# Weights and work buffers moved by 32 bytes in their partitions, and one row sum placed later, in a two-block transformer kernel

## The chip, the cores and the metric

The kernel runs on one core of one Trainium2 chip. The metric is the device time of one execution in microseconds, as the median of several executions. A profiled execution gives besides it a trace of every instruction on the engines: TensorE (PE, with its weight loads shown apart as PEld), VectorE (DVE), ScalarE (ACT), GpSimd (POOL) and SyncE (SP), which issues the DMAs.

## The reference: what is computed

Two small transformer stacks of two layers each, on 256 tokens of width 1024, in float32:

```
for i in range(2):                       # first block
    h = h + mixer_i(rms_norm(h))         # i=0: causal attention with rope (A); i=1: latent attention (B)
    h = h + conv_ffn(rms_norm(h))        # gelu(conv3(x @ w_gate)) * (x @ w_up) @ w_down, inner width 2816
h = rms_norm(h, norm_final)
for i in range(2):                       # second block
    x = x + mixer2_i(rmsnorm(x))         # i=0: pool_mixer (POOL); i=1: chunked attention with a bias (DD)
    x = x + conv_ffn_2(rmsnorm(x))       # silu in place of gelu
```

The pool mixer takes, for each of four groups of 256 channels, a trailing mean over 2, 4, 8 or 16 tokens minus the input, then a 256 by 256 linear map. The four FFNs are called F0, F1, F2 and F3; the order of the stages is A, F0, B, F1, POOL, F2, DD, F3.

## The kernel before, in words

All matrix products run on TensorE in `float32r`. A float32 number is split into a high part (what `float32r` keeps) and a low part (the rest), and each product is the sum of high times high, high times low and low times high. Activations lie channel by channel: `xT` (a part of the tile `gx`) holds the residual stream as 8 chunks of 128 channels by 256 tokens, and `xx` holds for each chunk `k` the high part and behind it the low part, 512 elements together.

**Weights.** The weights come from memory as 180-odd units of up to 128 by 2048 elements, in a fixed order (`unit_plan`). SyncE loads a unit into one of three buffers `raw`; ScalarE writes its high part into one of five buffers `whi` (`hi`, line 1165); VectorE subtracts and writes the low part into one of five buffers `wlo` (`lo`, line 1704); TensorE uses both.

**Matmuls.** Each matmul has a stationary operand (128 by 128, loaded by an LDWEIGHTS) and a moving one. In the FFNs and in half of the output projections the weights are stationary. `block_wide` (lines 458 and 460) is the pair of matmuls that does nearly all of this: the high weights against high and low activations together (512 moving elements), then the low weights against the high activations (256). Its moving operand is `xx` for the gate and up products, `hx` (the FFN's hidden activations, split the same way) for the down product, and `ox` (the attention output) for two of the four output units of each mixer. In one FFN there are 11 x 2 units x 8 chunks x 2 halves = 352 such pairs on `xx`, and 3 x 22 x 2 + 22 = 154 on `hx`; in each of the three attention mixers 32 on `ox`. That is 1408, 616 and 96 pairs in all. In the query, key and value products of A and DD (`high` and `low`, lines 671, 672 and 678) it is the other way round: the activations `xx` are stationary, and the weights `whi` or `wlo` are moving, 512 elements at a time, 3 x 192 = 576 matmuls. `three` (lines 417 to 419) is used elsewhere: three matmuls, of 256 moving elements as a rule.

**Order.** Every engine has its own program, written out by hand, and the engines meet at semaphores: `s_res` (a chunk pair of the residual stream is final), `s_xh` and `s_xl` (high and low part of a chunk of `xx` are written), `s_hs` (the row sums are split), `s_sum`, `s_sr`, `s_used` (TensorE has finished with a unit).

**The norm.** In an FFN the gate and up products run on activations without their norm, and the factor per token is multiplied in afterwards. The sum of squares over channels goes through `ssum` and its split copy `sx` (high by ScalarE line 1230, low by VectorE `low_sums`, line 1761) and is spread over all partitions by two matmuls with a matrix of ones (`spread_sums`, lines 512 to 514). VectorE reads the result from the bank `SB` (`norm_spread`, line 1767) and takes the inverse square root. A "row" of the FFN here is one index `i`: a gate unit and an up unit, 256 of the 2816 hidden channels.

**From POOL to F2.** While TensorE ends the pool mixer, VectorE and ScalarE finish the residual stream chunk by chunk: `normed(k)` (VectorE, line 2255) applies the final norm of the first block, `averages(g)` (line 2262) adds the pool mixer's output to chunks 2g and 2g+1, `split_x(F2, k)` writes chunk `k` of `xx` (ScalarE the high part, line 1168, VectorE the low part, line 1709). F2 starts on chunks 0 and 1 alone, gate and up, and goes on chunk by chunk.

**Addresses.** `sb` places tiles one behind another in each partition, in the order of the calls, at multiples of 32 bytes. In the built program `raw0` starts at byte 1152, a multiple of 64. All tiles but `gx` (8224 bytes) and `vec` (1756 bytes, 1760 with its filling) have a length that is a multiple of 64 up to the FFN's buffers, so the place of a tile within a 64-byte line changes only behind these two. Every slice that a wide matmul reads starts a multiple of 512 bytes behind its tile's start, so it has its tile's place in the line.

Of the kernel before, what the change touches and what calls it, by code (L numbers as in the profile page):

```python
# [100 lines left out]
def build(nc, dram, out):  # L101
    plan, first = unit_plan()
    N_UNITS = len(plan)
    with ExitStack() as ctx:
        def sb(name, shape, dt=F32, stack=ctx):
            return stack.enter_context(nc.sbuf_tensor(name, shape, dt))

        def sem(name):
            return ctx.enter_context(nc.semaphore(name))

# [38 lines left out]
        s_dv, s_ac = sem("s_dv"), sem("s_ac")  # L149

        raw = [sb(f"raw{i}", [128, UNIT]) for i in range(RAW)]
        whi = [sb(f"whi{i}", [128, UNIT], F32R) for i in range(RING)]
        wlo = [sb(f"wlo{i}", [128, UNIT], F32R) for i in range(RING)]
        gx = sb("gx", [128, KD + KD * S])
        xT = gx[:, KD:].rearrange("p (k s) -> p k s", k=KD)
        xx = sb("xx", [128, KD, 2, S], F32R)
        con = sb("con", [128, CON_N])
        vec = sb("vec", [128, VEC_N])
        ones = sb("ones", [128, 128])
        ones_r = sb("ones_r", [128, 128], F32R)  # L160
# [254 lines left out]
        def tensor_program(e):  # L415
# [47 lines left out]
            def across_wide(n, b, k, a, kk, start, stop):  # L463
                block_wide(n, b[:, 0, :], 0, k, a, kk, start, stop)
                return block_wide(n, b[:, 1, :], 1, k, a, kk, start, stop)
# [57 lines left out]
            def ffn(s):  # L523
                u = first[s]
                bg, bu = ffn_banks(s, 0), ffn_banks(s, 1)
                weights_here(u + 1)
                if s != F2:
                    e.wait_ge(s_res, n_res(s - 1, 1))
                if s == F2:
                    for k in (0, 1):  # L530
                        x_here(s, k)
                        across_wide(u, bg, k, xx, k, k == 0, False)
                    e.wait_ge(s_uu, 2)
                    for k in (0, 1):
                        across_wide(u + 1, bu, k, xx, k, k == 0, False)
                for k in range(2 if s == F2 else 0, KD):
                    x_here(s, k)
                    last = across_wide(u, bg, k, xx, k, k == 0, k == KD - 1)
                    if k == KD - 1:
                        last.then_inc(s_used, 1)  # L540
                    last = across_wide(u + 1, bu, k, xx, k, k == 0, k == KD - 1)
                    if k == KD - 1:
                        last.then_inc(s_used, 1)
                spread_sums(s)
                for i in range(1, 11):
                    n = u + 2 * i
                    bg, bu = ffn_banks(s, 2 * i), ffn_banks(s, 2 * i + 1)
                    weights_here(n)
                    if i >= 2:
                        e.wait_ge(s_gr, n_ff(s, i - 2))  # L550
                    for k in range(KD):
                        last = across_wide(n, bg, k, xx, k, k == 0, k == KD - 1)
                    last.then_inc(s_used, 1)
                    weights_here(n + 1)
                    if i >= 2:
                        e.wait_ge(s_ub, n_ff(s, i - 2))
                    else:
                        e.wait_ge(s_sr, LAYER[s] + 1)
                    for k in range(KD):
                        last = across_wide(n + 1, bu, k, xx, k, k == 0, k == KD - 1)  # L560
                    last.then_inc(s_used, 1)
                n = u + 22
                for c in range(4):
                    b = ffn_banks(s, 2 + c)
                    e.wait_ge((s_gr, s_ub)[c % 2], n_ff(s, 9 + c // 2))
                    if c == 3:
                        last_pair(s)
                        break
                    k0 = 0
                    for j, nk in enumerate((8, 8, 6)):  # L570
                        weights_here(n)
                        for k in range(nk):
                            if c == 0:
                                e.wait_ge(s_hl, n_ff(s, (k0 + k) // 2))
                            last = across_wide(n, b, k, hx, k0 + k, k0 + k == 0, k0 + k == NF - 1)
                        last.then_inc(s_used, 1)
                        n += 1
                        k0 += nk
# [1109 lines left out]
        def vector_program(e):  # L1688
# [548 lines left out]
            def pool_mixer():  # L2237
                s = POOL
                u = first[s]
                e.wait_ge(s_sum, s + 1)  # L2240
                sums = SB[:, 0, 0:4].rearrange("p (h w) -> p h w", h=2)
                e.tensor_scalar(va[:, 0:2], sums[:, :, 0], 1.0 / D, EPS, ALU.mult, ALU.add)
                kept(e.tensor_scalar(va[:, 2:4], sums[:, :, 1], 1.0 / D, None, ALU.mult))
                after_own()
                kept(e.scalar_tensor_tensor(out=va[:, 2:4], in0=va[:, 0:2], scalar=EPS, in1=va[:, 2:4], op0=ALU.mult,
                                            op1=ALU.add))
                rsqrt(va, ra, ta).then_inc(s_rc, 1)
                norm_diag(s, ra)
                norm_row(s, 0)
                e.wait_ge(s_rb, ROW[s])  # L2250
                e.wait_ge(s_xh, n_x(s, KD - 1))

                def normed(*chunks):
                    for k in chunks:
                        kept(e.scalar_tensor_tensor(out=xT[:, k, :], in0=xT[:, k, :], scalar=vcol("norm_final", k),
                                                    in1=rb[:, :], op0=ALU.mult, op1=ALU.mult))

                def averages(g):
                    xp = xT[:, 2 * g:2 * g + 2, :]
                    e.wait_ge(s_uu, g + 1)  # L2260
                    after_own()
                    e.tensor_tensor(xp, xp, pu[:, 2 * g:2 * g + 2, :], ALU.add).then_inc(s_res, 1)

                normed(0, 1, 2)
                averages(0)
                normed(3, 4)
                split_x(F2, 0)
                split_x(F2, 1)
                averages(1)
                normed(5)  # L2270
                split_x(F2, 2)
                split_x(F2, 3)
                normed(6, 7)
                averages(2)
                add_squares(F2, 1)
                split_x(F2, 4)
                split_x(F2, 5)
                averages(3)
                add_squares(F2, 2)
                split_x(F2, 6)  # L2280
                split_x(F2, 7)
                add_squares(F2, 3)
                fold_sums(F2)
                lo(u + 3)
                low_sums(F2)
                lo(u + 4)
# [177 lines left out]
```

## Time and profile before

| | us |
|---|---|
| median of 3 executions (1076.17 to 1076.5) | 1076.34 |
| profiled execution, its own time | 1077.13 |
| span of the profiled execution, first to last instruction | 1075.3 |
| PE busy / DVE busy / ACT busy | 1068.8 / 838.6 / 655.7 |

The span is what the trace covers; the execution's own time has 1.8 us around it. Busy time of PE is a sum over modelled ends of pipelined matmuls, so the time between the starts of two matmuls that follow each other says more than the duration of one. It is called a slot below. The granted TensorE clock is 1.000 of full speed over the span (its upper level, 2.4 GHz).

### The profile page before, as it was taken

The numbers are of one execution on the slowest core, as the hardware profiler recorded it, in microseconds if no ns is written. First come the engines' busy times: TensorE is split into PE (matmuls) and PEld (weight loads), VectorE is DVE, ScalarE is ACT, GpSimd is POOL, SyncE is SP. The second block draws the span as 40 slices with busy tenths as digits, with TensorE's granted clock in tenths as the row PEclk, the third lists the DMA queues.
The fourth block names the chain that finished last, engine by engine and source line by source line (L and its number), as shares of the span: only waits on it lengthen the run. The fifth ranks groups of instructions, "written<-read, shape, count | busy, mean of one in ns | idle before, by whom it ended". The sixth has DMA issues, their size and how long they took to land.

```text
span 1075.3 us, 16292 instructions
## 1 busy us (share of the span) xinstructions
PE 1068.8 (99%) x6536; PEld 934.0 (87%) x6536; DVE 838.6 (78%) x1364; ACT 655.7 (61%) x922; POOL 1.3 (0%) x8
## 2 busy tenths in 40 slices
PE   9999999999999999999999999999999999999998
PEld 7778888888898888888889888888877788888887
DVE  7985799877668778987767999776658768997852
ACT  7656567655467765766456577654456765776540
POOL 0000000000000000000000000000000000000000
PEclk9999999999999999999999999999999999999999
DMA  8553356555427154655552366555555434655530
GB/s 304 200 188 119 130 184 230 202 186 215 144 83 270 41 186 168 229 206 183 213 193 101 135 222 231 186 216 186 180 182 181 151 118 148 235 215 191 206 142 30
DMA packets 32092, 191.67 MB, mean 178 GB/s; under 512 B 4497, under 2 KB 6161, under 8 KB 12177
## 3 DMA queue, kind: packets, MB, share of 16 engines
q1 hardware_dynamic: 32016, 190.62, 49.9%
q8 instruction: 52, 0.85, 0.3%
q14 instruction: 24, 0.19, 0.0%
HBM read 189.56 MB, written 1.05 MB: 177 GB/s over the span
## 4 chain that ended last, share of the span: by engine, by line
PE 95%; DVE 2%; ACT 1%; DMA 1%; issue 1%; SPq 0%; DVEq 0%; ACTq 0%
PE banks L458 21%; PE TB L458 12%; PE SB L458 12%; PE banks L460 11%; PE SB L460 6%; PE TB L460 6%; PE banks L671 4%; PE banks L678 4%; PE banks L672 4%; PE banks L417 3%; PE banks L419 3%; PE banks L418 3%; PE banks L628 2%; PE TB L602 2%; PE SB L589 1%; DMA raw<-in_a_first 1%
## 5 line engine op out<-in xcount | busy, mean ns | idle before, releaser
L1704 DVE TENSOR_TENSOR wlo<-raw,whi 128x2048 fp32r<-128x2048 f32 (+2 forms) x180 | 395.9, 2201 | 76.2 <-ACT whi L1165 75.9
L1165 ACT ACTIVATE whi<-raw 128x2048 fp32r<-128x2048 f32 (+2 forms) x180 | 330.4, 1839 | 81.1 <-PE TB L460 25.6
L458 PE MATMUL banks<-xx,whi 128*128 128x512 f32 x752 | 262.1, 390 | 0.0
L460 PE MATMUL banks<-xx,wlo 128*128 128x256 f32 x752 | 212.0, 282 | 0.0
L458 PEld LDWEIGHTS banks<-xx,whi 128*128 128x128 f32 x752 | 141.1, 188 | 29.6
L460 PEld LDWEIGHTS banks<-xx,wlo 128*128 128x128 f32 x752 | 142.1, 189 | 0.0
L458 PE MATMUL TB<-xx,whi 128*128 128x512 f32 x336 | 117.7, 390 | 0.3 <-DVE xx L1709 0.3
L458 PE MATMUL SB<-xx,whi 128*128 128x512 f32 x320 | 111.8, 390 | 0.0
L460 PE MATMUL TB<-xx,wlo 128*128 128x256 f32 x336 | 94.7, 282 | 0.0
L458 PE MATMUL banks<-hx,whi 128*128 128x512 f32 x264 | 91.7, 391 | 0.0
L460 PE MATMUL SB<-xx,wlo 128*128 128x256 f32 x320 | 90.2, 282 | 0.0
L1250 ACT ACTIVATE ct<-gp,vec 128x256 f32<-128x256 f32 x88 | 48.2, 595 | 63.4 <-DVE gp L1871 63.4
L671 PE MATMUL banks<-whi,xx 128*128 128x512 f32 x192 | 78.6, 409 | 1.1 <-ACT whi L1657 1.1
L672 PE MATMUL banks<-whi,xx 128*128 128x512 f32 x192 | 76.3, 398 | 0.0
L458 PEld LDWEIGHTS TB<-xx,whi 128*128 128x128 f32 x336 | 63.0, 188 | 13.6 <-issue 0.5
L460 PE MATMUL banks<-hx,wlo 128*128 128x256 f32 x264 | 73.9, 280 | 0.0
L458 PEld LDWEIGHTS SB<-xx,whi 128*128 128x128 f32 x320 | 60.0, 188 | 12.6
L460 PEld LDWEIGHTS TB<-xx,wlo 128*128 128x128 f32 x336 | 63.5, 189 | 0.0
L458 PE MATMUL TB<-hx,whi 128*128 128x512 f32 x176 | 61.2, 391 | 0.0
L458 PE MATMUL SB<-hx,whi 128*128 128x512 f32 x176 | 61.2, 391 | 0.0
L460 PEld LDWEIGHTS SB<-xx,wlo 128*128 128x128 f32 x320 | 60.5, 189 | 0.0
L458 PEld LDWEIGHTS banks<-hx,whi 128*128 128x128 f32 x264 | 49.4, 187 | 10.8
(244 smaller groups left out, 1949.0 us busy)
## 6 DMA issues: line engine op xcount, KB each, us to landing
raw<-in_gate SPq DMA_DIRECT2D x44, 1024.0 KB, 4.8
raw<-in_up SPq DMA_DIRECT2D x44, 1024.0 KB, 4.8
raw<-in_down SPq DMA_DIRECT2D x32, 1024.0 KB, 4.8
raw<-in_down SPq DMA_DIRECT2D x16, 768.0 KB, 4.2
raw<-in_d_kq SPq DMA_DIRECT2D x8, 1024.0 KB, 4.9
raw<-in_a_kq SPq DMA_DIRECT2D x6, 1024.0 KB, 5.2
raw<-in_a_o SPq DMA_DIRECT2D x4, 1024.0 KB, 4.9
raw<-in_b_o SPq DMA_DIRECT2D x4, 1024.0 KB, 5.4
```

Source lines behind the costliest of these rows:

```text
L417: e.matmul(po, ah, bh, start=start, stop=False, skip_group_check=True)
L418: e.matmul(po, ah, bl, start=False, stop=False, skip_group_check=True)
L419: return e.matmul(po, al, bh, start=False, stop=stop, skip_group_check=True)
L458: e.matmul(po[:, 0:512], wh[:, k, sl], a[:, kk, :, :].rearrange("p w s -> p (w s)"), start=start, stop=stop, skip_group_check=True)
L460: return e.matmul(po[:, 0:256], wl[:, k, sl], a[:, kk, 0, :], start=False, stop=stop, skip_group_check=True)
L602: last = e.transpose(TB[:, a, c * 128:(c + 1) * 128], sc[:, a, c * 128:(c + 1) * 128], ident)
L671: e.matmul(po, xx[:, k, 0, sl], wh[:, k % 4, :], start=k == 0, stop=False, skip_group_check=True)
L672: e.matmul(po, xx[:, k, 1, sl], wh[:, k % 4, :], start=False, stop=False, skip_group_check=True)
L678: return e.matmul(slot_bank(s, i, h)[:, :], xx[:, k, 0, sl], wl[:, k % 4, :], start=False, stop=k == KD - 1, skip_group_check=True)
L1165: e.activation(whi[n % RING][:, 0:nk * w], raw[n % RAW][:, 0:nk * w], ACT.Copy).then_inc(s_hi, 1)
L1250: e.activation(ct[:, m, :], g[:, m, 0:S], ACT.Identity, scale=cw(0, 2 * i + m), bias=cb(2 * i + m)).then_inc(s_tap, 1)
L1704: e.tensor_tensor(wlo[n % RING][:, 0:nk * w], raw[n % RAW][:, 0:nk * w], whi[n % RING][:, 0:nk * w].bitcast(F32), ALU.subtract).then_inc(s ...
```

## The change

Three unused tiles of 32 bytes are allocated between others (`off_line`), which moves what lies behind them. In bytes from the last multiple of 64, as the built programs have it:

| tile | before | after |
|---|---|---|
| `raw0` to `raw2` | 0 | 0 |
| `whi0` to `whi4`, `wlo0` to `wlo4` | 0 | 32 |
| `gx`; `xT` in it | 0; 32 | 0; 32 |
| `xx`, `con` | 32 | 32 |
| `vec` | 32 | 0 |
| `ones`, `ones_r`, `sx`, `sq`, `ssum`, `rb`, `small`, `dg`, `crs`, `rtmp` | 0 | 32 |
| `hx`, `gp0`, the FFN's other buffers | 0 | 32 |
| `gp1` | 32 | 0 |
| `ox`, `vv`, `sc`, `pt`, `qT`, `kT` and the mixers' other buffers | 0 | 32 |

So for the wide matmuls the places of moving and stationary operand go, from (32, 0) to (32, 32) for `xx` against weights; from (0, 0) to (32, 32) for `hx` and `ox` against weights; and from (0, 32) to (32, 32) for weights against `xx`.

Apart from that, `spread_sums` of F2 is issued after the first chunk of the gate product of row 1 and no longer before that row, and VectorE does `normed(4)` after `averages(1)`.

```
+        def off_line(name):
+
+            sb(f"pad_{name}", [128, 8])
+
         raw = [sb(f"raw{i}", [128, UNIT]) for i in range(RAW)]
+        off_line("weights")
         whi = [sb(f"whi{i}", [128, UNIT], F32R) for i in range(RING)]
         wlo = [sb(f"wlo{i}", [128, UNIT], F32R) for i in range(RING)]
+        off_line("tokens")
         gx = sb("gx", [128, KD + KD * S])
         xT = gx[:, KD:].rearrange("p (k s) -> p k s", k=KD)
         xx = sb("xx", [128, KD, 2, S], F32R)
         con = sb("con", [128, CON_N])
+        off_line("moving")
         vec = sb("vec", [128, VEC_N])
...
-                spread_sums(s)
+                if s != F2:
+                    spread_sums(s)
                 for i in range(1, 11):
...
                     for k in range(KD):
                         last = across_wide(n, bg, k, xx, k, k == 0, k == KD - 1)
+                        if s == F2 and i == 1 and k == 0:
+                            spread_sums(s)
...
                 normed(0, 1, 2)
                 averages(0)
-                normed(3, 4)
+                normed(3)
                 split_x(F2, 0)
                 split_x(F2, 1)
                 averages(1)
-                normed(5)
+                normed(4, 5)
```

The order of TensorE at the end of the eight chunks of F2's row 0, before the change (the last four matmuls of row 0, the two of `spread_sums`, the first of row 1):

```order
L458 MATMUL banks<-xx,whi 128x512
L460 MATMUL banks<-xx,wlo 128x256
L458 MATMUL banks<-xx,whi 128x512
L460 MATMUL banks<-xx,wlo 128x256
L513 MATMUL SB<-sx,ones_r 128x256
L514 MATMUL SB<-sx,ones_r 128x256
L458 MATMUL banks<-xx,whi 128x512
```

And of the changed kernel, from the same place on (its `block_wide` has lines 465 and 467, its `spread_sums` line 520 and the one after it):

```order
L465 MATMUL banks<-xx,whi 128x512
L467 MATMUL banks<-xx,wlo 128x256
L465 MATMUL banks<-xx,whi 128x512
L467 MATMUL banks<-xx,wlo 128x256
L465 MATMUL banks<-xx,whi 128x512
L467 MATMUL banks<-xx,wlo 128x256
L465 MATMUL banks<-xx,whi 128x512
L467 MATMUL banks<-xx,wlo 128x256
L520 MATMUL SB<-sx,ones_r 128x256
```

Four matmuls of row 1 now stand ahead of the two that read `sx`.

The order of VectorE from the copy of the norm's row on, before (x3 and x2: that many in a row; 2255 is `normed`, 2262 `averages`, 1709 `split_x`):

```order
L1780 COPY rb<-TB 128x256
L2255 SCALAR_TENSOR_TENSOR gx<-gx,vec,rb 128x256 x3
L2262 TENSOR_TENSOR gx<-gx,pu 128x512
L2255 SCALAR_TENSOR_TENSOR gx<-gx,vec,rb 128x256 x2
L1709 SCALAR_TENSOR_TENSOR xx<-gx,vec,xx 128x256 x2
L2262 TENSOR_TENSOR gx<-gx,pu 128x512
L2255 SCALAR_TENSOR_TENSOR gx<-gx,vec,rb 128x256
L1709 SCALAR_TENSOR_TENSOR xx<-gx,vec,xx 128x256 x2
```

And of the changed kernel (2265, 2272 and 1719 are the same three):

```order
L1790 COPY rb<-TB 128x256
L2265 SCALAR_TENSOR_TENSOR gx<-gx,vec,rb 128x256 x3
L2272 TENSOR_TENSOR gx<-gx,pu 128x512
L2265 SCALAR_TENSOR_TENSOR gx<-gx,vec,rb 128x256
L1719 SCALAR_TENSOR_TENSOR xx<-gx,vec,xx 128x256 x2
L2272 TENSOR_TENSOR gx<-gx,pu 128x512
L2265 SCALAR_TENSOR_TENSOR gx<-gx,vec,rb 128x256 x2
L1719 SCALAR_TENSOR_TENSOR xx<-gx,vec,xx 128x256 x2
```

One `normed` stands two places later, behind the second `averages`. No instruction is added, removed or resized on any engine, and the orders are the same everywhere else.

## Rows read from the trace of the kernel before

**Rows 1.** The page's first part: span; busy us, share of the span, instructions.
```profile
span 1075.3 us, 16292 instructions
PE 1068.8 (99%) x6536; PEld 934.0 (87%) x6536; DVE 838.6 (78%) x1364; ACT 655.7 (61%) x922; POOL 1.3 (0%) x8
```
**Rows 2.** The chain of work that ended last, shares of the span by engine.
```profile
PE 95%; DVE 2%; ACT 1%; DMA 1%; issue 1%; SPq 0%; DVEq 0%; ACTq 0%
```
**Rows 3.** Waits of PE: total us, times, longest us.
```profile
PE SB L513 <- DVE sx L1761: 0.5, 1, 0.5
```
**Rows 4.** Groups of PE: out<-moving,stationary, count, busy us, mean ns, idle before.
```profile
L458 PE MATMUL banks<-xx,whi 128*128 128x512 f32 x752 | 262.1, 390 | 0.0
L458 PE MATMUL banks<-hx,whi 128*128 128x512 f32 x264 | 91.7, 391 | 0.0
L671 PE MATMUL banks<-whi,xx 128*128 128x512 f32 x192 | 78.6, 409 | 1.1 <-ACT whi L1657 1.1
```
**Rows 5.** Timeline of PE in F0 (start us, us): row 1's start, down's start, its last pair.
```profile
134.00 0.39 PE L458 MATMUL TB<-xx,whi 128*128 128x512 f32 x1
...
244.94 0.39 PE L458 MATMUL TB<-hx,whi 128*128 128x512 f32 x1
...
297.99 0.39 PE L458 MATMUL banks<-hx,whi 128*128 128x512 f32 x1
```
**Rows 6.** Timeline of PE in A's output projection, three pairs apart.
```profile
115.25 0.40 PE L458 MATMUL SB<-ox,whi 128*128 128x512 f32 x1
...
116.31 0.40 PE L458 MATMUL SB<-ox,whi 128*128 128x512 f32 x1
```
**Rows 7.** Timeline of PE at DD's start: the first and the 46th matmul.
```profile
773.10 0.40 PE L671 MATMUL banks<-whi,xx 128*128 128x512 f32 x1
...
783.60 0.40 PE L672 MATMUL banks<-whi,xx 128*128 128x512 f32 x1
```
**Rows 8.** Timeline of PE in B, weights moving against `ox`: 17 slots apart.
```profile
331.00 0.39 PE L419 MATMUL banks<-whi,ox 128*128 128x512 f32 x1
...
334.85 0.39 PE L418 MATMUL banks<-wlo,ox 128*128 128x512 f32 x1
```
**Rows 9.** Timeline of PE, 256 moving: 3 slots apart in F0, 6 apart in POOL.
```profile
300.00 0.28 PE L419 MATMUL banks<-hx,wlo 128*128 128x256 f32 x1
...
300.36 0.28 PE L419 MATMUL banks<-hx,wlo 128*128 128x256 f32 x1
...
580.77 0.28 PE L419 MATMUL banks<-whi,xx 128*128 128x256 f32 x1
...
581.48 0.28 PE L419 MATMUL banks<-whi,xx 128*128 128x256 f32 x1
```
**Rows 10.** Timelines of PE and DVE round `spread_sums` of F2.
```profile
599.80 0.28 PE L460 MATMUL banks<-xx,wlo 128*128 128x256 f32 x1
600.55 0.35 PE L513 MATMUL SB<-sx,ones_r 128*128 128x256 f32 x1 [0.47 <-DVE sx L1761]
600.86 0.39 PE L458 MATMUL banks<-xx,whi 128*128 128x512 f32 x1
...
606.42 0.39 PE L458 MATMUL SB<-xx,whi 128*128 128x512 f32 x1
...
599.99 0.42 DVE L1761 TENSOR_TENSOR sx<-ssum,sx 128x256 fp32r<-128x256 f32 x1
...
602.55 0.41 DVE L1767 TENSOR_SCALAR rtmp<-SB 128x256 f32<-128x256 f32 x1
```
**Rows 11.** Timelines of PE, DVE and ACT at the start of F2.
```profile
588.74 0.47 PE L458 MATMUL TB<-xx,whi 128*128 128x512 f32 x1 [0.31 <-DVE xx L1709]
...
588.12 0.88 DVE L1709 SCALAR_TENSOR_TENSOR xx<-gx,vec,xx 128x256 fp32r<-128x256 f32 x2
...
590.17 0.88 DVE L1709 SCALAR_TENSOR_TENSOR xx<-gx,vec,xx 128x256 fp32r<-128x256 f32 x2 [0.18 <-ACT xx L1168]
...
587.44 0.91 ACT L1168 ACTIVATE xx<-gx,vec 128x256 fp32r<-128x256 f32 x2 [0.28 <-DVE gx L2262]
```

More of the change, by code:

```diff
@@ L106, in sb, with off_line @@
             return stack.enter_context(nc.sbuf_tensor(name, shape, dt))
+        def off_line(name):
+            sb(f"pad_{name}", [128, 8])
         def sem(name):
@@ L151, in build @@
         raw = [sb(f"raw{i}", [128, UNIT]) for i in range(RAW)]
+        off_line("weights")
         whi = [sb(f"whi{i}", [128, UNIT], F32R) for i in range(RING)]
         wlo = [sb(f"wlo{i}", [128, UNIT], F32R) for i in range(RING)]
+        off_line("tokens")
         gx = sb("gx", [128, KD + KD * S])
@@ L157, in build @@
         con = sb("con", [128, CON_N])
+        off_line("moving")
         vec = sb("vec", [128, VEC_N])
@@ L543, in ffn @@
                         last.then_inc(s_used, 1)
-                spread_sums(s)
+                if s != F2:
+                    spread_sums(s)
                 for i in range(1, 11):
@@ L552, in ffn @@
                         last = across_wide(n, bg, k, xx, k, k == 0, k == KD - 1)
+                        if s == F2 and i == 1 and k == 0:
+                            spread_sums(s)
                     last.then_inc(s_used, 1)
@@ L2265, in pool_mixer @@
                 averages(0)
-                normed(3, 4)
+                normed(3)
                 split_x(F2, 0)
@@ L2269, in pool_mixer @@
                 averages(1)
-                normed(5)
+                normed(4, 5)
                 split_x(F2, 2)
```

## The prediction, made before the changed kernel was run

> **What bounds the kernel now.** I read the page's first part, then the chain, then the waits of TensorE. TensorE is busy for 1068.8 of 1075.3 us [rows 1], and 95% of the chain that ended last is TensorE's own work [rows 2]. Its waits for other engines are single ones of 1.1 us at most [rows 3, 4]; the largest inside the change's reach is 0.5 us for `sx` [rows 3]. So nothing but TensorE's own rate, and two places round F2, can move the time: what VectorE, ScalarE and the DMA queue gain or lose by new addresses is hidden unless it is several per cent of a stage. The groups give the forms of the matmuls, but their durations are modelled (390, 391 and 409 ns, which overlap) [rows 4]; the slots between starts are what the time consists of, so I take them from the timeline.
>
> **The slots, by place in the 64 bytes (moving, stationary).**
> - `xx` against weights, (32, 0): rows 1 to 10 of F0 are 10 x 2 x 8 x 2 = 320 pairs, from 134.00 to 244.94 us [rows 5]: 346.7 ns a pair.
> - `hx` against weights, (0, 0): 153 pairs from 244.94 to 297.99 [rows 5]: 346.7 ns a pair.
> - `ox` against weights, the same form and also (0, 0): 3 pairs in 1.06 us [rows 6]: 353.3 ns.
> - weights against `xx`, 512 moving, (0, 32): 45 slots from 773.10 to 783.60 [rows 7]: 233.3 ns.
> - weights against `ox`, 512 moving, (0, 0): 17 slots from 331.00 to 334.85 [rows 8]: 226.5 ns.
> - 256 moving: 120 ns at (0, 0) and 118 ns at (0, 32) [rows 9].
>
> Three things are to be seen. The steady slots differ by steps of 6.7 ns. The same places and the same form have given two of them (`hx` and `ox`), so the place is not all that decides. And the one clean difference at one form is that of the 512-wide single matmuls: 6.8 ns less where both operands start at the same place than where they don't. No matmul of the kernel before has (32, 32), which is what all wide ones get. Its price must be bounded from its neighbours.
>
> **The change, part by part.**
>
> *The queries, keys and values of A and DD*, 576 matmuls of 512 moving elements, go from (0, 32) to (32, 32). If what counts is whether the two operands stand alike, they take the slot of rows 8: 576 x 6.8 ns = 3.9 us less. Lower bound of the cost: that. Upper bound: nothing gained, 0. I take the first, since rows 7 and 8 are the only two of one form that differ in nothing else that I can name. TensorE waits for nobody there but at A's start (1.1 us in all of line 671 [rows 4]), so the gain would be kept.
>
> *The pairs on `xx`*, 1408 of them, go from (32, 0) to (32, 32), *those on `hx`*, 616, and `ox`, 96, from (0, 0). `xx` and `hx` have the same 346.7 ns at unlike and at like places, so I cost both at nothing. The bounds are one step to each side. `ox` shows that one step up exists: 1408 x 6.7 = 9.4 us for `xx` alone. One step down has not been seen for a pair; it would be 2024 x 6.7 = 13.5 us for `xx` and `hx`.
>
> *`spread_sums` of F2.* The last matmul ahead of it starts at 599.80, so TensorE is free at 599.92, a slot of about 118 ns later; the sums start at 600.55 and row 1 at 600.86 [rows 10]. The stall is 0.63 us, and what is late is VectorE's `sx`, from 599.99. Two pairs of row 1 (0.69 us) now go ahead: TensorE would be at the sums at 600.61, and `sx` is there by 600.55. What has been done ahead is saved: 0.63 us, and up to 0.69 us if TensorE comes a little earlier. Behind the sums, VectorE's reading of `SB` (602.55, done by 602.96) releases the up product of row 1, which wrote `SB` first at 606.42 and will ask for it 0.7 us earlier, at 605.7: 2.8 us of margin [rows 10].
>
> *`normed(4)` later.* F2's first matmul (588.74) waited for chunk 0 of `xx`, whose low part began at 588.12; ScalarE's high part began at 587.44, two in 0.91 us, so it was there at about 587.9 [rows 11]. VectorE can begin about 0.15 to 0.2 us earlier, and TensorE with it. But the sums of F2 start when `sx` is ready, not when TensorE is, and VectorE's work up to `sx` is the same in sum. So these 0.15 us end in a wait for `sx`, and I count them at nothing. The cost on the other side: chunk 2's low part, before from 590.17, comes up to 0.44 us (half of a 0.88 us row) later, ready by 591.1; TensorE wants it eight pairs after its start, 588.6 + 2.8 = 591.4 [rows 11]. Hidden, with 0.3 us to spare; without that cover it costs at most 0.2 us. If VectorE's chain to `sx` ends 0.2 us later, so does the gain shrink to 0.5. I take 0.7 for both edits together, bounds 0.4 and 0.9.
>
> **Sum.** 0.7 + 3.9 = 4.6 us. The profiled execution took 1077.13 us with a span of 1075.3, so it would be 1072.5, with a span of 1070.7. The median is 0.8 us below the profiled one: 1076.34 - 4.6 = 1071.7 us. Of a change of this kernel, 0.2% (2.2 us) is about what a measurement can tell from none.
>
> **Rivals.**
> - *Only the sums' place counts: 1075.6 us.* The slots don't depend on the place by 32 bytes, rows 7 and 8 differ for another reason (rows 5 and 6 differ at the same places, which speaks for it), and 0.7 us is left. The Trainium skill (SBUF — State Buffer, Specifications) says that SBUF has 16-byte lines and that crossing to a new one costs; by that rule 32 bytes are two whole lines and every read crosses as many as before, so it gives this same result. The trace neither shows nor excludes it.
> - *A step down for the pairs: 1071.7 - 13.5 = 1058.2 us.* If (32, 32) is a place of its own in which the loads disturb the moving stream less. For it speaks that a pair takes 346.7 ns while the 256-wide slot alone can be 118: there is room. Against it: no pair of rows 5 and 6 has it. The Trainium skill (TensorE: Matmul & The Clock Gate, Wait — 56ns, not 53.3ns?) gives start to start as columns over 2.4 GHz and about 2.5 ns; that would be 325 ns for a pair, so by this page as well there is room, and the trace is 22 ns above it.
> - *Weights off the 64-byte start as stationary operand cost: 1086 us, slower.* The mechanism is read from rows 7 and 8 the other way: not that the places are unlike, but that the stationary operand starts at 32 makes a 512 slot 6.8 ns longer; rows 9 give 2 ns less for a 256 slot. Then each of the 2120 pairs becomes 4.8 ns longer, 10.2 us, nothing is won in A and DD, and the 0.7 us go off: 1085.8. A form of it is that `xx` takes the longer slot that `ox` has: 1076.34 + 9.4 - 0.7 - 3.9 = 1081.1. It decides as soon as a pair on `xx` is over 2 ns longer. Against it: `xx` and `hx` don't differ, but there the stationary operand is at 0 in both, so they say nothing of it.
>
> **How the numbers follow.** Forecast (A and DD gain, pairs as they are, between 1070 and 1074): 0.36. Only the sums' place: 0.2. A step down for pairs: 0.2; some of their cases, with one of `xx` and `hx` alone, lie between 1058 and 1068. Slower by a pair's longer slot: 0.24. Faster by over 0.2% is the first and the third, 0.56 less a little for a gain in A and DD of under 1.5 us: 0.55. Within 0.2%: 0.2 and that little, 0.21. Slower: 0.24. The range from 1057.5 to 1081.5 leaves out the worse half of the slower case (about 0.13) and what would be better than one step down (0.05). The likeliest case's own range is 1070 to 1074.
>
> **What would show it.** In the changed trace: F0's rows 1 to 10 in 110.9 us and the 153 pairs on `hx` in 53.05 (pairs unchanged); DD's first 45 slots in 10.2 us in place of 10.5 (places alike); 0.31 us from the sums' first matmul to the next of row 1 with no wait of over 0.1 us ahead of it. The prediction is wrong if a pair's slot moves at all, since 1 ns in it is 2.1 us; if DD's slots stay at 233; or if TensorE begins to wait in A or DD, where ScalarE and VectorE would then be the bound.

## The result, and the profile after

The changed kernel takes 1086.13 us (median of 4 runs, 1086.03 to 1086.84) against 1076.38 us before (4 runs, 1076.17 to 1076.5): ratio 1.0093, 95% interval 1.0081 to 1.0106. It is 9.75 us slower, where 4.6 us less was forecast and 1081.5 us was the top of the range. The profiled execution of the kernel before was 0.75 us above its median (1077.13), so the two traces differ by 8.9 us only. All ratios compare executions at a granted clock of 0.998 or more; one of e10's ten ran at 0.851, took 1160.53 us and is left out of them.

The page's first part and the chain of the changed kernel, to be read against [rows 1, 2]:

```profile
span 1084.2 us, 16292 instructions
PE 1078.5 (99%) x6536; PEld 933.0 (86%) x6536; DVE 839.0 (77%) x1364; ACT 656.1 (61%) x922; POOL 1.3 (0%) x8
...
PE 96%; DVE 2%; ACT 1%; issue 0%; DMA 0%; SPq 0%; ACTq 0%; DVEq 0%
```

The span grew by 8.9 us and TensorE's busy time by 9.7. VectorE and ScalarE are busy for 0.4 us more each. The list has no new wait of note; the waits of PE (us in total, times, longest), against [rows 3]:

```profile
PE SB L672 <- DVE ones L2298: 1.1, 1, 1.1
PE banks L681 <- ACT whi L1667: 0.7, 1, 0.7
PE SB L1013 <- DVE small L1941: 0.4, 2, 0.2
PE TB L465 <- DVE xx L1719: 0.2, 1, 0.2
```

The wait for `sx` is gone, as meant. So the time is in TensorE's own slots, and there the groups show the pairs longer (395 ns in place of 390 and 391) and the matmuls of A and DD as they were [rows 4]:

```profile
L465 PE MATMUL banks<-xx,whi 128*128 128x512 f32 x752 | 266.4, 395 | 0.0
...
L465 PE MATMUL banks<-hx,whi 128*128 128x512 f32 x264 | 93.2, 395 | 0.0
...
L681 PE MATMUL banks<-whi,xx 128*128 128x512 f32 x192 | 78.4, 408 | 0.7 <-ACT whi L1667 0.7
```

The slots come from the timeline of PE: row 1's start, the down product's start and its 154th pair, in F0 and then in F3; last DD's first and 46th matmul. They answer to [rows 5, 7].

```profile
133.18 0.40 PE L465 MATMUL TB<-xx,whi 128*128 128x512 f32 x1
...
246.25 0.40 PE L465 MATMUL TB<-hx,whi 128*128 128x512 f32 x1
...
300.31 0.40 PE L465 MATMUL banks<-hx,whi 128*128 128x512 f32 x1
...
907.53 0.40 PE L465 MATMUL TB<-xx,whi 128*128 128x512 f32 x1
...
1019.18 0.39 PE L465 MATMUL TB<-hx,whi 128*128 128x512 f32 x1
...
1072.56 0.39 PE L465 MATMUL banks<-hx,whi 128*128 128x512 f32 x1
...
780.94 0.40 PE L681 MATMUL banks<-whi,xx 128*128 128x512 f32 x1
...
791.44 0.39 PE L682 MATMUL banks<-whi,xx 128*128 128x512 f32 x1
```

- F0: 320 pairs on `xx` in 113.07 us and 153 on `hx` in 54.06: 353.3 ns each, 6.7 more than before. The stretch of 473 pairs is 3.14 us longer. F1 is alike (3.15), and F2 from row 1's third pair on, behind the sums in both kernels (3.11).
- F3: 111.65 and 53.38 us, 348.9 ns each: one third of that step, 1.05 us.
- DD: 45 slots in 10.50 us, 233.3 ns, unchanged.

The four stretches sum to 10.5 us. The rest of the program is 1.6 us shorter (0.8 of it ahead of F0's row 1, 0.6 between F1's last pair and the third pair of F2's row 1): 8.9 us.

### The profile page after: what moved, and what is told of

Same layout as the page of the kernel before. It is cut to its first block, busy times and chain, and to the rows that moved or that the text cites. A ratio compares the mean times of both kernels' runs of the same rounds, so it can differ in the third digit from the quotient of the medians.

```text
span 1084.2 us, 16292 instructions
## 1 busy us (share of the span) xinstructions
PE 1078.5 (99%) x6536; PEld 933.0 (86%) x6536; DVE 839.0 (77%) x1364; ACT 656.1 (61%) x922; POOL 1.3 (0%) x8
## 3 DMA queue, kind: packets, MB, share of 16 engines
HBM read 189.56 MB, written 1.05 MB: 176 GB/s over the span
## 4 chain that ended last, share of the span: by engine, by line
PE 96%; DVE 2%; ACT 1%; issue 0%; DMA 0%; SPq 0%; ACTq 0%; DVEq 0%
PE banks L465 21%; PE TB L465 12%; PE SB L465 12%; PE banks L467 11%; PE TB L467 6%; PE SB L467 6%; PE banks L681 4%; PE banks L688 4%; PE banks L682 4%; PE banks L424 3%; PE banks L425 3%; PE banks L426 3%; PE banks L638 2%; PE TB L612 2%; PE SB L599 1%; PE banks L757 1%
## 5 line engine op out<-in xcount | busy, mean ns | idle before, releaser
L465 PE MATMUL banks<-xx,whi 128*128 128x512 f32 x752 | 266.4, 395 | 0.0
```

Source lines behind the costliest of these rows:

```text
L465: e.matmul(po[:, 0:512], wh[:, k, sl], a[:, kk, :, :].rearrange("p w s -> p (w s)"), start=start, stop=stop, skip_group_check=True)
```

## The experiments

e1, e2, e4, e6 and e7 keep the order of before, e3 keeps its addresses; all the others have the order of the changed kernel. None leaves work out. I describe an address by the **distance**: the start of the moving buffer less that of the stationary one, in bytes of a partition, modulo 256. The starts follow from adding up the buffers in the order of their declarations; every slice that a pair reads begins a multiple of 256 bytes behind its buffer's start, so a distance holds for a whole stretch. Before, weights against `xx` are at 32, against `hx` and `ox` at 0; in the changed kernel all three are at 64, because one pad more lies between the weights and `xx` and two more between the weights and `hx` or `ox`, not because of where in a line each stands.

"Pair" is the slot of a pair on `xx` in F0, from the same two rows as above, 320 pairs apart, in the one execution of each kernel that has a trace; other stages can differ, as the text says. Ratios are to the kernel before, timed on the same chip (1076.2 to 1076.4 us).

| kernel | distance `xx`; `hx`, `ox` | pair, ns | median, us | ratio, 95% |
|---|---|---|---|---|
| before | 32; 0, 0 | 346.7 | 1076.38 | 1 |
| changed | 64; 64, 64 | 353.3 | 1086.13 | 1.0081 to 1.0106 |
| e1 weights alone | 64; 32, 32 | 348.9 | 1079.01 | 1.0015 to 1.0033 |
| e2 buffers behind `con` alone | 32; 32, 32 | 346.7 | 1073.95 | 0.997 to 0.9989 |
| e3 order alone | 32; 0, 0 | 346.7 | 1075.84 | 0.9989 to 1.0006 |
| e4 `xx` moved to 64-byte starts | 64; 64, 64 | 353.3 | 1085.15 | 1.0069 to 1.0097 |
| e5 = e2 + e3 | 32; 32, 32 | 346.7 | 1073.75 | 0.9966 to 0.9986 |
| e6 pads ahead of `wlo`, `gx` and `vec` | high 96, low 64 | 353.3 | 1088.85 | 1.0102 to 1.013 |
| e7 weights 16 bytes in, by buffer | mixed | 350.4 | 1082.72 | 1.0045 to 1.0076 |
| e8 changed, `ox` 32 on | 64; 64, 96 | 353.3 | 1088.55 | 1.0099 to 1.0127 |
| e9 | 128; 128, 128 | 351.1 | 1083.81 | 1.0056 to 1.0086 |
| e10 all 64 on | 32; 32, 32 | 346.7 | 1073.67 | 0.9966 to 0.9986 |
| e11 | 160; 160, 160 | 346.7 | 1074.77 | 0.9978 to 0.9996 |
| e12 | high 16, low 144 | 348.9 | 1079.47 | 1.0018 to 1.0041 |
| e13 changed, `ox` at 32 | 64; 64, 32 | 348.9 | 1081.17 | 1.0028 to 1.0058 |
| e14 changed, one pad less | 32; 32, 32 | 346.7 | 1073.89 | 0.9966 to 0.9986 |
| e15 | 224; 224, 224 | 353.3 | 1088.37 | 1.0095 to 1.0125 |
| e16 | high 48, low 176 | 344.5 | 1069.86 | 0.9928 to 0.9964 |
| e17 | 48; 48, 48 | 350.0 | 1081.33 | 1.0038 to 1.0064 |
| e18 | 176; 176, 176 | 353.3 | 1087.80 | 1.0092 to 1.0123 |

### The change taken apart

e1 adds the pads ahead of `whi` and `gx` alone:
```diff
+        off_line("weights")
         whi = [sb(f"whi{i}", [128, UNIT], F32R) for i in range(RING)]
         wlo = [sb(f"wlo{i}", [128, UNIT], F32R) for i in range(RING)]
+        off_line("tokens")
```


> Kernel before, with only the weights' high and low parts moved by 32 bytes; xx stays at 32, hx and ox at 0, no order changed. Theory S (the stationary operand's place decides, the moving one's does not): pairs on xx and on hx both take 352 to 353 ns in place of 346.7, matmuls of three with weights stationary 117.8 in place of 120, weights moving in A and DD stay at 233.3; in all 1086.8 us, the changed kernel and the 0.7 us of its order. Theory T (both operands must be off the 64-byte start): pairs on xx 352 to 353, those on hx (0, 32) stay at 346.7; about 1083.5 us. Theory M (the moved hx and ox and the other buffers cost it): 1076.4 us.

e2 adds the pad ahead of `vec` alone, e3 the new place of the sums and of `normed(4)` alone:
```diff
+        off_line("moving")
         vec = sb("vec", [128, VEC_N])
```


> Kernel before, with only vec and all behind it moved by 32 bytes (hx, ox, the FFN's and mixers' buffers at 32, weights and xx as before). Theory S: pairs on xx and hx stay at 346.7 ns, 1076.4 us, at most 0.3 us more for the few matmuls of B in which ox is stationary. Theory T: the same. Theory M: about 1086 us, with pairs on hx at 352 ns.

```diff
-                spread_sums(s)
+                if s != F2:
+                    spread_sums(s)
...
+                        if s == F2 and i == 1 and k == 0:
+                            spread_sums(s)
```


> Kernel before, with only the changed order: spread_sums of F2 behind the first chunk of row 1, normed(4) behind averages(1). All theories of places: 1075.7 us, 0.7 us less (0.4 to 0.9), with the sums' first matmul starting when it did, at 600.5 us of the span, and two pairs of row 1 ahead of it. If VectorE's chain to sx comes later by what it lost at chunk 2: 1076.1 us.

The timeline of PE in e1 (F0, first two rows) and in e2 (F0):

```profile
132.77 0.40 PE L464 MATMUL TB<-xx,whi 128*128 128x512 f32 x1
...
244.42 0.39 PE L464 MATMUL TB<-hx,whi 128*128 128x512 f32 x1
```
```profile
132.43 0.39 PE L463 MATMUL TB<-xx,whi 128*128 128x512 f32 x1
...
243.37 0.39 PE L463 MATMUL TB<-hx,whi 128*128 128x512 f32 x1
...
296.41 0.39 PE L463 MATMUL banks<-hx,whi 128*128 128x512 f32 x1
```

e1: 348.9 ns on `xx`, 2.2 more, but 346.7 on `hx`, though the weights are 32 bytes on for both. So it isn't the weights' own place that costs. None of the three times expected came. The traced execution took 1077.43 us, 1.6 less than the median, so the 348.9 ns need not be the slot of all ten. e2 is 2.3 us faster than before with the same 346.7 ns: its gain lies in the shorter forms. With `hx` and `ox` at distance 32 a single 256 slot on `hx` went from 119.8 to 116.7 ns (264 of them), one on `ox` from 123.8 to 121.2 (408), and a pair on `ox` from 353.3 to 347.1 (96): 0.8 + 1.1 + 0.6 = 2.5 us (means over neighbouring starts).

e3 shows what the order is worth. Its PE, and VectorE, at the start of F2's row 1, against [rows 10], behind F0's row 1:

```profile
133.63 0.39 PE L458 MATMUL TB<-xx,whi 128*128 128x512 f32 x1
...
599.34 0.28 PE L460 MATMUL banks<-xx,wlo 128*128 128x256 f32 x1
599.85 0.50 PE L458 MATMUL banks<-xx,whi 128*128 128x512 f32 x1 [0.23 <-DVE wlo L1707]
600.19 0.28 PE L460 MATMUL banks<-xx,wlo 128*128 128x256 f32 x1
...
600.66 0.28 PE L513 MATMUL SB<-sx,ones_r 128*128 128x256 f32 x1
...
600.89 0.40 PE L458 MATMUL banks<-xx,whi 128*128 128x512 f32 x1
...
597.52 2.28 DVE L1707 TENSOR_TENSOR wlo<-raw,whi 128x2048 fp32r<-128x2048 f32 x1
```

The sums no longer wait, but the pairs moved ahead of them do: row 1's gate weights get their low part from 597.52 to 599.80, and TensorE, free at 599.46, starts at 599.85. Before, this was hidden, since TensorE stood at the sums until 600.55 [rows 10]. The third pair of row 1 starts at 600.89, before at 600.86 + 2 x 0.347 = 601.55; that is 0.66 us less, of which 0.37 was there at F0's row 1 (133.63, before 134.00), where the programs are the same. The order is worth 0.3 us, and its time can't be told from no change. In the changed kernel row 1 starts late in the same way, by 0.18 us (its first pair at 605.36, behind a matmul of about 118 ns that starts at 605.06), too little to stand in the list of waits.

### Place or distance

e4 leaves the weights and moves `xx` and what is behind it (pads ahead of `xx` and ahead of `ones`); e5 is e2 and e3 together; e6 was meant to move `wlo` and not `whi`.
```diff
         xT = gx[:, KD:].rearrange("p (k s) -> p k s", k=KD)
+        off_line("x")
         xx = sb("xx", [128, KD, 2, S], F32R)
```


> Kernel before, with xx, con and vec moved to a multiple of 64 bytes and all else left at one, so that all operands of wide matmuls are at (0, 0). Theory S: weights moving against xx in A and DD take 226.5 ns in place of 233.3 (576 matmuls, 3.9 us), pairs on xx stay at 346.7 and the products of 256, 288 and 384 moving in B and POOL shift by a few ns: 1072.5 us. Theory T: A and DD stay at 233.3 and nothing else moves: 1076.4 us. If the pairs on xx took the other slot seen at (0, 0), that of ox: plus 9.4 us, 1082 us.

> The two parts of the change that gained alone, together: vec and all behind it moved by 32 bytes, and the order round F2; weights and xx as before. Theory U (a pair of operands at unlike places, 32 bytes apart modulo 64, has one rhythm of 346.7 ns, whatever went before; at like places there are several, and the one that a stage falls into stays): the gains add, 2.3 and 0.5 us, 1073.4 us, every pair on xx, hx and ox at 346.7. Rival, that the gain of the moved buffers lies in VectorE's or ScalarE's work: the same total, but then pairs and matmuls of three would not account for it.

```diff
         whi = [sb(f"whi{i}", [128, UNIT], F32R) for i in range(RING)]
+        off_line("low")
         wlo = [sb(f"wlo{i}", [128, UNIT], F32R) for i in range(RING)]
+        off_line("tokens")
```


> As the moved buffers alone, but the weights' low parts at 32 too: in a pair the 512 slot has stationary high parts at an unlike place, and the 256 slot stationary low parts at a like one. If the disturbance comes from the load that runs under the moving stream (low parts load under the 512 stream), the 512 slot is the one that changes. If the operand's own place decides, the 256 slot alone changes. Theory U with any like operand enough: pairs at 348.9 or 353.3 ns, 1078 to 1086 us; with both loads needed: 346.7, 1074.0 us.

PE in e4, F0:

```profile
132.72 0.40 PE L464 MATMUL TB<-xx,whi 128*128 128x512 f32 x1
...
245.79 0.40 PE L464 MATMUL TB<-hx,whi 128*128 128x512 f32 x1
```

353.3 ns with both operands on 64-byte starts: the loss of the changed kernel, without its weights moved (four executions, 1084.03 to 1086.18 us). e5, which is the changed kernel without the two pads round the weights, keeps 346.7 and is faster than before. e6 is the slowest of all (means of 231.7 and 121.7 ns for the two slots, before 228.3 and 118.3): both matmuls of a pair become longer. This doesn't tell the operands apart: modulo 64 only the low parts were shifted against `xx`, but modulo 256 the high parts went from 32 to 96 as well as the low ones from 32 to 64.

e7 and e8 were made to tell places apart. e7 took the weights 16 bytes in, with tiles of `UNIT + 16` elements. This was unclean: the tiles are then no multiple of 256 bytes and the distance changes from buffer to buffer (80, 144, 208, 16). Its slots are mixed too, from 346.7 ns (A's `ox`) to 351.2. e8 adds a pad of 32 bytes ahead of `ox` to the changed kernel.
```diff
-        whi = [sb(f"whi{i}", [128, UNIT], F32R) for i in range(RING)]
+        whi = [sb(f"whi{i}", [128, UNIT + 16], F32R)[:, 4:4 + UNIT] for i in range(RING)]
```


> As the moved buffers alone, but the weights' high and low parts start 16 bytes behind a multiple of 64, so 16 bytes ahead of xx, hx and ox. If lines of 16 bytes are what counts, all places are alike and pairs go as at like places: 348.9 to 353.3 ns, 1078 to 1086 us. If the distance modulo 64 counts, it is neither alike nor 32: a slot of its own, between 340 and 353 ns; theory U in its simplest form (anything but alike is one rhythm) says 346.7 and 1074.0 us.

```diff
         att_mem = ExitStack()
+        sb("pad_att", [128, 8], F32, att_mem)
         ox = sb("ox", [128, KD, 2, S], F32R, att_mem)
```


> The changed kernel with ox and the mixers' other buffers moved back to 0, so that ox alone is at an unlike place; xx and hx against weights are at (32, 32) as in the changed kernel. If history decides at like places: ox runs at 346.7 ns, and the pairs on xx in F0 and F1, which follow on it, come into the rhythm of 348.9 that they had with the weights alone moved, and hx after them; F2 follows on POOL and stays at 353.3; about 1081 us. If places alone decide: xx and hx stay at 353.3 in F0 to F2 and only ox gains, 0.6 us: 1085.5 us.

The pad moves `ox` and the mixers' other buffers behind it, and none of those that an F stage reads. e8's `ox` pairs (distance 96) took 350.2 ns, which no theory then held had given, and its F3 took 353.3 ns a pair where the changed kernel has 348.9, with the same addresses in F3. With that the theory of places like and unlike fell, and distance, with a memory of what went before, was put in its place. e9 to e12 test the distance: three pads ahead of `xx` (e9), two ahead of `whi` (e10), four ahead of `gx` (e11); e12 puts the weights into one tile each, 16 bytes in.

```diff
+        off_line("x0")
+        off_line("x1")
+        off_line("x2")
         xx = sb("xx", [128, KD, 2, S], F32R)
```


> New theory V: what counts is the distance from the stationary operand's start to the moving one's, modulo 128 bytes (pairs so far: 32 gave 346.7 ns in every run; 0 gave 346.7 or 353.3; 64 gave 348.9 or 353.3; 96 gave 350.0), not whether they stand alike modulo 64. Here, with the order of the change, all wide matmuls are at distance 0 modulo 128. V: pairs on xx and hx at 346.7 or 353.3 (one of the two), weights moving against xx in A and DD at 226.5 in place of 233.3 (3.9 us), as the 17 slots of B before. With pairs at 346.7: 1072 us; at 353.3: 1086 us. The theory of like places modulo 64: pairs at 353.3 or 348.9 and A and DD at 233.3 as when xx was moved to 0, 1085 us.

```diff
+        off_line("w0")
+        off_line("w1")
         whi = [sb(f"whi{i}", [128, UNIT], F32R) for i in range(RING)]
```


> The moved buffers and the order, and weights, xx and all behind moved on by 64 bytes together: the distances are those of that kernel (32 for pairs), the places modulo 128 are the others. Theory V: every pair at 346.7 ns, 1073.7 us. If the place modulo 128 of either operand decides and not the distance, pairs go to 348.9 or more: over 1078 us.

```diff
+        off_line("t0")
+        off_line("t1")
+        off_line("t2")
+        off_line("t3")
         gx = sb("gx", [128, KD + KD * S])
```


> The moved buffers and the order, with 128 bytes more between the weights and gx: distance 160, which is 32 modulo 128. Theory V: every pair at 346.7 ns, 1073.7 us. If the distance counts modulo 256: a slot not seen so far, or one of 348.9 to 353.3, 1078 us and more.

```diff
+        his, los = (sb(name, [128, RING * UNIT + 32], F32R) for name in ("whi", "wlo"))
+        whi = [his[:, 4 + i * UNIT:4 + (i + 1) * UNIT] for i in range(RING)]
+        wlo = [los[:, 4 + i * UNIT:4 + (i + 1) * UNIT] for i in range(RING)]
```


> The moved buffers and the order, with the weights 16 bytes further on (all high parts behind each other in one tile, all low parts in another, so that each starts 16 bytes behind a multiple of 128): distance 16. Theory V has no number for it: between 346.7 and 353.3 ns a pair, 1073 to 1086 us. If only whole steps of 32 bytes count (the distance rounded down), it goes as distance 0, 346.7 or 353.3.

PE in e9, F0:

```profile
133.04 0.39 PE L466 MATMUL TB<-xx,whi 128*128 128x512 f32 x1
...
245.40 0.40 PE L466 MATMUL TB<-hx,whi 128*128 128x512 f32 x1
```

e10 is the clean one: every operand of a pair 64 bytes on, distance 32 kept, and time and slots are those of e5 to 0.1 us. It is also the changed kernel with the weights alone 32 bytes further on: the two pads ahead of `gx` are both ahead of the weights here, so `gx`, `xx` and all behind stand at the changed kernel's own addresses. PE in e10, F0:

```profile
132.77 0.39 PE L465 MATMUL TB<-xx,whi 128*128 128x512 f32 x1
...
243.71 0.39 PE L465 MATMUL TB<-hx,whi 128*128 128x512 f32 x1
```

346.7 ns in place of 353.3, and 12.5 us less. e9 missed both values expected: 128 gives 351.1 ns where 0 gave 346.7 on `hx` [rows 5] and 353.3 on `ox` [rows 6], so those two aren't alike; 128 is no period. e11 (160) has the 346.7 ns of 32, by another rhythm of the slots (230 and 117, 229 and 118, 228 and 118 ns, where 32 has 228 and 118, 228 and 119, 229 and 118).

### The cause by one pad, and the memory

e14 is the changed kernel without the pad ahead of `gx`; the weights stay where the change put them. e13 is the changed kernel with `ox` at distance 32 (a pad of 56 elements ahead of it, which moves the mixers' other buffers too). e15 has six pads ahead of `gx` and the weights as before.
```diff
-        off_line("tokens")
         gx = sb("gx", [128, KD + KD * S])
```


> The changed kernel without its second pad: weights still at 32 modulo 64, xx and all behind 32 bytes less far on, so that every pair is at distance 32. If the distance is the cause: all pairs at 346.7 ns, 1073.7 us, 12.4 us less than the changed kernel, by one pad. If weights off a multiple of 64 cost anything by themselves: more than 1075 us.

```diff
         att_mem = ExitStack()
+        sb("pad_att", [128, 56], F32, att_mem)
         ox = sb("ox", [128, KD, 2, S], F32R, att_mem)
```


> The changed kernel with ox and the mixers' other buffers moved on by 224 bytes, so that ox is at distance 32 from the weights, as it was with the weights alone moved; xx and hx stay at distance 64. If what went before decides at distance 64: ox at 346.7 ns, then xx in F0, F1 and F3 at 348.9, hx after it too; F2, which follows on POOL, open; 1080 to 1082 us. If not: 353.3 stays in F0 to F2 and only ox and the matmuls of three on it gain: 1085 us.

```diff
+        off_line("t0")
...
+        off_line("t5")
         gx = sb("gx", [128, KD + KD * S])
```


> The moved buffers and the order, with 192 bytes more between the weights and gx: distance 224, which is 32 bytes the other way modulo 256 (96 modulo 128). If only the size of the distance counts: 346.7 ns a pair, 1073.7 us. If it goes as the 96 modulo 128 that ox had once: 350.0 ns, about 1081 us.

PE in e14, F0:

```profile
132.82 0.39 PE L464 MATMUL TB<-xx,whi 128*128 128x512 f32 x1
...
243.77 0.39 PE L464 MATMUL TB<-hx,whi 128*128 128x512 f32 x1
...
296.81 0.39 PE L464 MATMUL banks<-hx,whi 128*128 128x512 f32 x1
```

One pad of 32 bytes less, 12.2 us less, as expected: 346.7 ns for all pairs on `xx` and `hx`, in a kernel with the weights 32 bytes into the 64. Here the weights stay and the moving operands go 32 bytes back; in e10 the moving operands stay and the weights go 32 bytes on. Either takes the loss away, so the cause of the slower result is the distance and not the place of one operand. PE in e13, F0 and F2, row 1's start (in F2 its third pair, behind the sums) and the down product's:

```profile
133.16 0.40 PE L466 MATMUL TB<-xx,whi 128*128 128x512 f32 x1
...
244.81 0.39 PE L466 MATMUL TB<-hx,whi 128*128 128x512 f32 x1
...
601.98 0.40 PE L466 MATMUL banks<-xx,whi 128*128 128x512 f32 x1
...
714.34 0.39 PE L466 MATMUL banks<-hx,whi 128*128 128x512 f32 x1
```

Here F0 takes 348.9 ns and F2 353.3 (318 pairs in 112.36 us), at one distance of 64 and with nothing changed but `ox` and the mixers' buffers behind it, which no F stage reads. The time, 1081.17 us, is the one expected if history decides. At 64 two steady rhythms exist, and F0, with its own addresses unchanged, went from one to the other by a change ahead of it: that is shown; what exactly decides it is not. The four executions of e13 lie within 0.4 us and those of the changed kernel within 0.8, where one stage's other rhythm would be about 2.1 us (473 x 4.4 ns), so in these two it isn't chance from one execution to the next. e15 adds 224, at 353.3 ns in all four F stages, which neither case expected: as high as 64, and unlike 32 or 160. But A's `ox` pairs ran there at 346.7 ns and B's at 353.3, so 224 has two rhythms as well, as 0 has [rows 5, 6].

### Which distance is low

e16 is e12 with one more pad ahead of `gx`. Its expectation and that of e12 call the distance 48 and 16; that is right for the high parts only. Their two tiles are not a multiple of 256 bytes long, so the low parts stood at 176 and 144. I saw this only afterwards; e17 (both tiles 128 bytes longer, both distances 48) and e18 (four more pads, both 176) take the mixture apart.

```diff
+        off_line("t")
         gx = sb("gx", [128, KD + KD * S])
```


> The kernel of distance 16 with 32 bytes more ahead of gx: distance 48, between 32 (346.7 ns, one rhythm) and 64 (348.9 or 353.3). If 32 is the bottom of a slope: about 348 to 350 ns a pair, 1077 to 1081 us. If there is a lower slot still, it would be here: under 346.7.

```diff
-        his, los = (sb(name, [128, RING * UNIT + 32], F32R) for name in ("whi", "wlo"))
+        his, los = (sb(name, [128, RING * UNIT + 64], F32R) for name in ("whi", "wlo"))
```


> The version with the weights 16 bytes into one tile each took 1069.9 us with 344.4 ns a pair, but its distances (moving start less stationary start, modulo 256 bytes) were 48 for the high parts and 176 for the low ones, since its two tiles are not a multiple of 256 bytes long. Here both tiles are 128 bytes longer and both distances are 48. If 48 for the high parts makes the low slot and the low parts count little: 344.4 ns a pair and 1069 to 1071 us, as there. If the distance counts modulo 128 alone: the same. If it was the mixture of 48 and 176 that was low: another slot, 346.7 ns or more, and 1074 us or more.

> As the one with both distances at 48, with 128 bytes more before the tokens, so that both are 176. If the distance counts modulo 128 for this place: 344.4 ns a pair and 1069 to 1071 us, as with 48. If it was 48 for the high parts that was low, and modulo 256 counts (0 and 128 gave 346.7 and 351.1 ns): another slot than 344.4, by the nearest measured ones (160: 346.7, 224: 353.3) 346.7 to 349 ns and 1074 to 1079 us.

PE in F0 of e16, e17 and e18:

```profile
132.56 0.39 PE L465 MATMUL TB<-xx,whi 128*128 128x512 f32 x1
...
242.79 0.39 PE L465 MATMUL TB<-hx,whi 128*128 128x512 f32 x1
```
```profile
135.50 0.40 PE L465 MATMUL TB<-xx,whi 128*128 128x512 f32 x1
...
247.49 0.39 PE L465 MATMUL TB<-hx,whi 128*128 128x512 f32 x1
```
```profile
132.21 0.40 PE L469 MATMUL TB<-xx,whi 128*128 128x512 f32 x1
...
245.27 0.40 PE L469 MATMUL TB<-hx,whi 128*128 128x512 f32 x1
```

344.5, 350.0 and 353.3 ns: 344.4 was one of the values expected for each of the last two, and came in neither. So neither 48 nor 176 is low by itself; only the mixture was. (e17's trace is of its slowest execution, 1083.72 us; it starts F0's row 1 at 135.50, where all other kernels of the table do by 134.0, and the slots behind are steady.) The slot of a pair depends on the distances of its high and of its low part together (or, the same thing said otherwise, also on that between the two weight buffers, 128 in e12 and e16 and 0 elsewhere but in e6 and e7). e16 beats both kernels: 6.5 us less than before and 16.3 less than the changed one. Against e5 it gains 2.2 ns on each of 2120 pairs, 4.7 us, and has 3.9 of them in the median; one of its four executions took 1073.77 us, the others 1070.0 or less.

## Why the prediction was wrong

- **Where the time can come from** held: TensorE's slots alone; VectorE, ScalarE and the waits gave nothing.
- **The step that failed** is "`xx` and `hx` have the same 346.7 ns at unlike and at like places, so I cost both at nothing". That 346.7 ns stood at two distances, 32 and 0, was read as freedom from addresses. The change sent both to a third, 64, which no row of before showed. The upper bound named there, one step of 6.7 ns up, was the truth for three of the four F stages, and not for `xx` alone but for `hx` too: 2024 x 6.7 = 13.5 us at most, of which F3's smaller step (2.2 ns) leaves about 11.2, 10.5 in the stretches measured. It was priced for `xx` alone (9.4 us) and given too little chance.
- **The variable was wrong.** I sorted by each operand's place in 64 bytes. e4 (both at a 64-byte start, slow), e14 (weights 32 in, fast) and e10 (fast with `xx` and `hx` at the changed kernel's addresses) show that the place by itself does nothing. What the change altered was the distance, and a pad ahead of several buffers changes it only towards the buffers on its other side.
- **The rival of 1085.8 us** came within 0.4 us of the time with a mechanism that fell: weights 32 bytes in as the stationary operand cost nothing in e14, nor on `hx` in e1. Its 4.8 ns on each pair stand against 6.7 in three stages and 2.2 in one. The nearness is chance.
- **A and DD, 3.9 us less**: not found, the second term that failed. DD's first 45 slots are 233.3 ns before and after; over all neighbouring starts under 250 ns apart, A and DD both have 233.2 before, and 233.4 and 233.3 after. What made the 226.5 ns of rows 8 short was not that the operands stood alike: both still do in the changed kernel, and the same 17 slots take 233.5 ns there.

```profile
331.08 0.39 PE L426 MATMUL banks<-whi,ox 128*128 128x512 f32 x1
...
335.05 0.40 PE L425 MATMUL banks<-wlo,ox 128*128 128x512 f32 x1
```

- **The order, 0.7 us**: 0.3, below its lower bound of 0.4. The working asked when `sx` and the `up` product's bank were ready, and not whether row 1's weights were, which the old wait had covered.
- **The pages cited.** The Trainium skill (SBUF — State Buffer, Specifications) with its 16-byte lines was weighed as: 32 bytes change nothing. By that rule 1075.6 us; the trace disagrees, as one pad of 32 bytes between e14 and the changed kernel is 12.2 us. By the Trainium skill (TensorE: Matmul & The Clock Gate, Wait — 56ns, not 53.3ns?) there was room below 346.7 ns; e16's 344.5 used 2.2 ns of it, still over 19 ns above the 325 ns estimated from the page's rule. The same skill (SBUF — State Buffer, Who interferes with whom) says that PE never waits on anyone; no run here tests that against another engine's accesses. What the runs show is that its rate depends on where its own two operands lie: the kernels at 344.5 and at 353.3 ns (e16, e18) differ in addresses alone.

That the loads of the stationary operand and the reads of the moving one meet in the same part of the memory is the explanation I find likeliest for this dependence. It was argued, not shown: no run has one without the other. Open, too, is which property of the pair of distances (high 48, low 176) makes the low slot, and whether others are lower.

## What to carry to other kernels

Where TensorE is the bound and streams float32r pairs, an allocation moved by a few bytes anywhere between weights and moving operands can change TensorE's rate, here from 344.5 to 353.3 ns a pair, 18 us in 1080 (e16 against e18). Read that rate from the starts of some hundred matmuls, sort by the distance of the two operands' starts and not by either's place, and treat a distance that the trace hasn't shown as unknown in both directions, and one that it has shown as known for that stage only, since 0, 64 and 224 each ran at two rates. Where a stall is filled with work moved ahead, ask when that work's own inputs come: the old stall may have hidden them.

## What the runs showed that I had not expected

- The steady slots lie on steps of about 1.1 ns and multiples (344.5, 346.7, 348.9, 350.0, 351.1, 353.3 ns a pair) and hold for hundreds of pairs; the single slots repeat with a short period (at distance 64: 237 and 118, 234 and 123, 231 and 117 ns, three pairs of 353.3 on average).
- At distance 64 the same addresses ran at 348.9 or 353.3 ns: by stage in the changed kernel and in e13, and by the place of `ox` and the mixers' other buffers (e8 and e13 against the changed kernel). The spread of e1's ten runs, 1076.8 to 1080.05 us, is wider than that of before (1075.7 to 1077.2), and so is that of e4's four; this would fit such a choice from one execution to the next (352 pairs x 4.4 ns are 1.5 us), but each has a trace of one execution only.
- In e6 (high parts at 96, low parts at 64) both matmuls of the pair were longer than at 32, by 3.4 ns each.
